# One more pair of gate tiles in the seven-product form, one third of the attention steps without a gate slice, and a new place for the copies of turned probabilities in those steps

## The reference

```
z = x @ w["w_in"]                     # 1024 x 6416
gq, gk, gv, gr, ga, sq, sk, sv, mq, gl = jnp.split(z, SPLIT_AT, axis=-1)
o_b = swa_banded(q, k, v, w["swa_sinks"])      # 8 heads of 64, own chunk and 2 before
o_c = mem_attention(mq, mem_k, mem_v)          # 4 heads of 128 into 256 memory tokens
g_a, g_b, g_c = jnp.split(jax.nn.sigmoid(gl + w["b_gate"]), 3, axis=-1)
mix = (g_a * y_a + g_b * y_b + g_c * y_c) @ w["w_o"]
x = layer_norm(ALPHA * x + mix, w["ln1_g"], w["ln1_b"])
x = layer_norm(ALPHA * x + conv_ffn(x), w["ln2_g"], w["ln2_b"])
```

## Time and profile before

| what | value |
|---|---|
| time, median of 3 runs | 1750.6 us (1750.44 to 1751.13) |
| the profiled execution's own time | 1747.55 us |
| its span | 1745.4 us |
| granted TensorE clock, mean | 0.998 |
| TensorE busy with matmuls | 1722.2 us, 99% |
| VectorE busy | 1088.5 us, 62% |
| ScalarE busy | 757.8 us, 43% |
| GpSimd busy | 219.0 us, 13% |

### The profile page before, as it was taken

One profiled execution on the slowest core, in us unless ns is written; L12 is line 12 of the kernel. 1 busy time (PEld: TensorE's weight loads), 2 busy tenths in 40 slices (PEclk: granted clock), 3 DMA queues, 4 the chain that ended last, 5 costly groups with the idle time before them and its releaser, 6 DMA issues.

```text
span 1745.4 us, 31878 instructions
## 1 busy us (share of the span) xinstructions
PE 1722.2 (99%) x12185; PEld 1667.6 (96%) x12185; DVE 1088.5 (62%) x1556; ACT 757.8 (43%) x1366; POOL 219.0 (13%) x319
## 2 busy tenths in 40 slices
PE   9999999999999999999999999999999999999997
PEld 8999999999998899899998889999999999999997
DVE  6644432666645766566664788777777777554474
ACT  6433332445434555563340255444455444433342
POOL 0000000000001200000000033333333331002011
PEclk9999999999999999999999999999999999999999
DMA  5333328422436311125463232222222213875672
GB/s 165 111 109 109 122 77 256 117 71 76 138 93 206 105 46 49 52 90 147 141 203 96 80 85 85 86 73 73 73 73 74 87 58 130 269 250 171 210 234 72
DMA packets 191505, 207.84 MB, mean 119 GB/s; under 512 B 21525, under 2 KB 152406, under 8 KB 191414
## 3 DMA queue, kind: packets, MB, share of 16 engines
q1 hardware_dynamic: 189558, 200.60, 36.9%
q0 software_dynamic: 1856, 5.99, 1.0%
HBM read 157.43 MB, written 48.53 MB: 118 GB/s over the span
## 4 chain that ended last, share of the span: by engine, by line
PE 65%; DVE 3%; issue 1%; SPq 1%; DMA 1%; ACT 1%; POOL 0%; ACTq 0%; POOLq 0%; DVEq 0%
PE banks L1681 24%; PE banks L1179 10%; PE banks L1180 10%; PE banks L1181 10%; PE banks L1638 5%; PE banks L1475 1%; PE banks L1492 1%; PE banks L1487 1%; PE banks L1455 1%; PE banks L1460 1%; DMA kpad<-gates_scratch 1%; PE banks L1649 0%; DVE wo L2809 0%; PE banks L1615 0%; SPq L797 0%
## 5 line engine op out<-in xcount | busy, mean ns | idle before, releaser
L1681 PE MATMUL banks<-x_free_r,a_hi 128*128 128x256 f32 x1232 | 226.8, 282 | 0.8 <-DVE a_lo L2919 0.5
L1179 PE MATMUL banks<-act_hi,w_hi 128*128 128x352 f32 (+1 forms) x672 | 223.7, 333 | 2.3 <-DVE w_lo L2448 1.4
L1181 PE MATMUL banks<-act_hi,w_lo 128*128 128x352 f32 (+1 forms) x672 | 218.0, 324 | 0.0
L1180 PE MATMUL banks<-act_lo,w_hi 128*128 128x352 f32 (+1 forms) x672 | 217.9, 324 | 0.0
L1681 PEld LDWEIGHTS banks<-x_free_r,a_hi 128*128 128x128 f32 x1232 | 190.1, 188 | 1.3 <-DVE x_free_r L2945 0.7
L1681 PE MATMUL banks<-xs_hi,a_hi 128*128 128x274 f32 x616 | 178.8, 290 | 1.7 <-DVE xs_lo L2945 1.1
L1681 PE MATMUL banks<-xs_lo,a_hi 128*128 128x274 f32 x616 | 178.4, 290 | 0.0
L1681 PE MATMUL banks<-xs_hi,a_lo 128*128 128x274 f32 x616 | 178.3, 289 | 0.0
L1681 PE MATMUL banks<-x_free_r,a_lo 128*128 128x256 f32 x616 | 173.4, 281 | 0.0
L1180 PE MATMUL banks<-h_lo,w_hi 128*128 128x384 f32 (+1 forms) x448 | 147.3, 329 | 0.0
L1179 PE MATMUL banks<-h_hi,w_hi 128*128 128x384 f32 (+1 forms) x448 | 146.8, 328 | 0.0
(11 more groups left out here) (355 smaller groups left out, 4324.0 us busy)
## 6 DMA issues: line engine op xcount, KB each, us to landing
w_raw<-in_w_down SPq DMA_DIRECT2D x112, 256.0 KB, 3.5
w_raw<-in_w_in SPq DMA_DIRECT2D x80, 256.0 KB, 3.9
gate_in<-gates_scratch SPq DMA_DIRECT2D x24, 529.0 KB, 3.6
h_keep<-conv SPq DMA_DIRECT2D x22, 530.0 KB, 2.7
gates_scratch<-zu SPq DMA_DIRECT2D x11, 1058.0 KB, 7.1
w_raw<-in_w_up SPq DMA_DIRECT2D x44, 256.0 KB, 3.9
x_free<-in_w_up SPq DMA_DIRECT2D x44, 256.0 KB, 3.7
h_raw<-h_keep SPq DMA_DIRECT2D x22, 384.0 KB, 5.2
```

Of the source, the lines that this page charges most:

```text
L1179: pe.matmul(out, hi, b_hi, start=start, stop=False)
L1180: pe.matmul(out, hi, b_lo, start=False, stop=False)
L1181: return pe.matmul(out, lo, b_hi, start=False, stop=stop)
L1681: last = pe.matmul(out, a[j][:, k, :], x[s][j][:, k, :], start=fresh and k == 0 and n_ == 0, stop=k == 3 and n_ == 2, skip_group_check=True)
```

## The change

Three things are changed together.

1. NZ goes from 11 to 12: gate tiles 22 and 23 are computed as a twelfth unit of the z stage. `Z_LAST` carries the parity of the last unit, and the tiles behind it use the banks of the other parity.
2. The attention stage has 18 gate slices instead of 24. Six steps, `ATT_BARE`, all with a mem unit (j % 3 = 2), have none; the slices stand in the others in order, so a tile's split comes after its third slice wherever that stands. The loops over i = 1 and 2 on the three engines are written out, since the steps differ.
3. Around a bare step k the copies of unit k's turned probabilities stand one step earlier in the programs: VectorE makes its half between the mask add and the maximum of unit k+1, ScalarE its half ahead of the exponentials of unit k+1.

```diff
-NZ = 11
+NZ = 12
+Z_LAST = (NZ - 1) % 2
-Z_GATES = (12, 14, 6, 8)
+Z_GATES = (12, 14, 6, 8, 22)
+ATT_BARE = ((0, 5), (1, 2), (1, 5), (2, 2), (2, 5), (3, 2))
+ATT_FILL = [(i, j) for i in range(5) for j in range(6) if (0, 3) <= (i, j) <= (4, 2) and (i, j) not in ATT_BARE]
...
-        z_pair(NZ - 1, 0)
+        z_pair(NZ - 2, 0)
+        z_pair(NZ - 1, Z_LAST)
...
         def gate_slice_b(i, j, beside=None):
 
-            if j % 3 == 0:
-                tile_start(i + (T_GATE_B // 2 + j // 3 - 1), 1 - j // 3)
-            proj_slice(i * 6 + (PS_GATE_B + j - 3), (PS_GATE_B + j - 3) % 2, 1 - j // 3, j % 3, beside)
+            s = att_fill(i, j)
+            if s is None:
+                return
+            f = s // 3
+            if s % 3 == 0:
+                tile_start((T_GATE_B + f) // 2, f % 2)
+            proj_slice(PS_GATE_B + s, (PS_GATE_B + s) % 2, f % 2, s % 3, beside)
...
         att_steps(0, True, False)
-        with pe.Fori(1, NT // 2 - 1) as i:
+        for i in range(1, NT // 2 - 1):
             att_steps(i, False, False)
...
                     gate_out_b(i, j)
-                probs_out(k, P)
+                if (i, j) not in ATT_BARE:
+                    probs_out(k, P)
...
                 values_out(k, j % 3, c, w)
-                if j % 3 == 2:
-                    split_hi(i + (T_GATE_B // 2 + b), 1 - b)
+                next_gate(i, j)
+                if (i, j + 1) in ATT_BARE:
+                    probs_out(k + 1, P)
...
-        def max_unit(k, swa, r, par, w, nk, band):
+        def max_unit(k, swa, r, par, w, nk, band, turned=None):
...
+                if turned is not None:
+                    probs_out(turned, P)
                 dve.wait_ge(q.masked, swa + 1)
...
-                if not (first and j < 2):
+                if not (first and j < 2) and (i, j) not in ATT_BARE:
                     probs_out(k, P)
                 n = j + 2
                 w, nk = (DEC, P + DEC) if last and n >= 6 else (P, 2 * P)
-                max_unit(k + 2, i * 4 + (n - n // 3), n % 3, n % 2, w, nk, None if last and n >= 6 else mask)
+                max_unit(k + 2, i * 4 + (n - n // 3), n % 3, n % 2, w, nk, None if last and n >= 6 else mask,
+                         k + 1 if (i, j + 1) in ATT_BARE else None)
```

More of the change, by code:

```diff
@@ L81 @@
 T_GATE_B = T_MQ + 10
-T_MERGE = T_MQ + 18
-T_WO = T_MQ + 30
-T_FFN = T_MQ + 38
+T_MERGE = T_MQ + 16
+T_WO = T_MQ + 28
+T_FFN = T_MQ + 36
 PW0, PW1, PBG, PW2, PCB, PGN, PHI = 0, NF * 2, NF * 4, NF * 4 + 24, NF * 6 + 24, NF * 8 + 24, NF * 8 + 25
@@ L475, in program @@
     BRANCHES = (2, 0, 1)
-    PS_Z, PS_G, PS_GA, PS_FILL, PS_MQ, PS_MQ_B, PS_MK, PS_MV, PS_GATE_B, PS_END = 6, 9, 11, 15, 57, 60, 63, 65, 67, 91
+    PS_Z, PS_G, PS_GA, PS_FILL, PS_MQ, PS_MQ_B, PS_MK, PS_MV, PS_GATE_B, PS_END = 6, 9, 11, 15, 57, 60, 63, 65, 67, 85
     q = Semaphores(sem)
@@ L516, in fill_slice, with att_fill @@
         return sum(FILL_SLICES[:t]) + places.index(place) if place in places else None
+    def att_fill(i, j):
+        return ATT_FILL.index((i, j)) if (i, j) in ATT_FILL else None
     def z_count(n, j):
@@ L568, in raw_count @@
         if par:
-            return 384 if isinstance(c, int) and c < 2 else c * 32 + 352
+            return 448 if isinstance(c, int) and c < 2 else c * 32 + 416
         return 32 * (W0 + 1) if isinstance(c, int) and c < 2 else c * 16 + 32 * (W0 + 1)
@@ L824, in _ @@
             mem_tile(n_)
-        last = gate_loop(T_GATE_B // 2, 16, 4, gate_st2, PS_GATE_B)
+        last = gate_loop(T_GATE_B // 2, 16, 3, gate_st2, PS_GATE_B)
         def merge_tile(turn, slot, br, mp):
@@ L851, in _ @@
         merge_tile(T_MERGE // 2, 1, BRANCHES[1], 0)
-        last(3, (0,))
+        last(2, (0,))
         sp.wait_ge(q.staged, 2 * NT + 2)
@@ L855, in _ @@
         gate_back(0)
-        last(3, (1,))
+        last(2, (1,))
         for s in range(3):
-            sp.wait_ge(gate_stored[s], 16 * (10 + NFILL))
+            sp.wait_ge(gate_stored[s], 16 * (8 + NFILL))
         for k in range(12):
@@ L1297, in _ @@
         z_pair(1, 1, 1)
-        with pe.Fori(1, NZ // 2) as i:
+        with pe.Fori(1, (NZ - 1) // 2) as i:
             z_pair(i * 2, 0)
             z_pair(i * 2 + 1, 1)
-        z_pair(NZ - 1, 0)
+        z_pair(NZ - 2, 0)
+        z_pair(NZ - 1, Z_LAST)
         tile_start(1, 0)
@@ L1306, in _ @@
         for gi in range(3):
-            proj_slice(PS_Z + gi, 3 + 4 * (gi % 2), 0, gi)
+            proj_slice(PS_Z + gi, bank_a(1 - Z_LAST, gi % 2), 0, gi)
         for s in range(2):
@@ L1917, in _ @@
         z_window(1, 1)
-        with act.Fori(1, NZ // 2) as i:
+        with act.Fori(1, (NZ - 1) // 2) as i:
             z_window(i * 2, 0)
             z_window(i * 2 + 1, 1)
+        z_window(NZ - 2, 0)
         for k in range(3):
             for s in range(2):
-                z_snap(NZ - 1, 0, s, k)
+                z_snap(NZ - 1, Z_LAST, s, k)
         split_hi(1, 0, used=(q.prod_mm[1], z_count(NZ - 1, 0)))
         for s in range(2):
-            z_snap(NZ - 1, 0, s, 3)
+            z_snap(NZ - 1, Z_LAST, s, 3)
         split_hi(1, 1, used=(q.prod_mm[1], z_count(NZ - 1, 4)))
@@ L1937, in _ @@
         for gi in range(3):
-            gate_out(PS_Z + gi, 3 + 4 * (gi % 2), gi, gate_st, 0)
+            gate_out(PS_Z + gi, bank_a(1 - Z_LAST, gi % 2), gi, gate_st, 0)
             if gi == 1:
@@ L2079, in gate_out_b, with next_gate @@
         def gate_out_b(i, j):
-            gate_out(i * 6 + (PS_GATE_B + j - 3), (PS_GATE_B + j - 3) % 2, j % 3, gate_st2, i * 2 + (1 + NFILL + j // 3))
+            s = att_fill(i, j)
+            if s is not None:
+                gate_out(PS_GATE_B + s, (PS_GATE_B + s) % 2, s % 3, gate_st2, 2 + NFILL + s // 3)
+        def next_gate(i, j):
+            s = att_fill(i, j)
+            if (i, j) == (0, 2):
+                split_hi(T_GATE_B // 2, 1)
+            elif s is not None and s % 3 == 2:
+                split_hi((T_GATE_B + s // 3 + 2) // 2, s // 3 % 2)
         def att_steps(i, first, last):
@@ L2109, in _ @@
         att_steps(0, True, False)
-        with act.Fori(1, NT // 2 - 1) as i:
+        for i in range(1, NT // 2 - 1):
             att_steps(i, False, False)
@@ L2161, in _ @@
         for gi in range(3):
-            act.wait_ge(gate_stored[gi], 16 * (10 + NFILL))
+            act.wait_ge(gate_stored[gi], 16 * (8 + NFILL))
         act.wait_ge(q.k_turned, 1)
@@ L2571, in _ @@
         z_window(1, 1)
-        with dve.Fori(1, NZ // 2) as i:
+        with dve.Fori(1, (NZ - 1) // 2) as i:
             z_window(i * 2, 0)
             z_window(i * 2 + 1, 1)
+        z_window(NZ - 2, 0)
         for k in range(3):
             for s in range(2):
-                z_combine(NZ - 1, 0, s, k)
+                z_combine(NZ - 1, Z_LAST, s, k)
             if k == 0:
@@ L2781, in att_steps @@
                     split_lo(T_GATE_B // 2, 0)
-                if j % 3 == 2:
-                    split_lo(i + (T_GATE_B // 2 + j // 3), 1 - j // 3)
+                s = att_fill(i, j)
+                if (i, j) == (0, 2):
+                    split_lo(T_GATE_B // 2, 1)
+                elif s is not None and s % 3 == 2:
+                    split_lo((T_GATE_B + s // 3 + 2) // 2, s // 3 % 2)
         def branch_lo(place):
@@ L2793, in _ @@
         att_steps(0, True, False)
-        with dve.Fori(1, NT // 2 - 1) as i:
+        for i in range(1, NT // 2 - 1):
             att_steps(i, False, False)
```

## The result

| | before | after |
|---|---|---|
| median | 1751.1 us (5 executions, 1750.4 to 1754.9) | 1777.9 us (5 executions, 1772.5 to 1779.2) |
| profiled execution: own time, span | 1747.55, 1745.4 us | 1778.02, 1775.9 us |
| mean granted clock | 0.998 | 0.992 |

The account below looks back on a forecast made before the run. TensorE, busy 99% of the span, was taken as the bound. Added z unit 20.65, removed slices -23.9 and six waits of 3.5 gave +17.8 us on 1750.6: 1768.4 us, with 1761 to 1777 for 8 in 10.

Parts of the forecast that it names:

- the likeliest case: TensorE waits 2.8 to 4.2 us at the products behind each bare step, at full clock; chance 0.68.
- The z unit: In the z stage, one more unit bound by its matmuls adds 20.65 us, its loads and store costed at nothing.
- Six slices: In the attention stage, six gate slices of 3.98 to 3.99 us removed from TensorE: -23.9 us.
- The chain of 12.99 us: Handovers up to VectorE's copy of unit k+1; TensorE arrives at 9.77 and waits 3.22 us per bare step.
- GpSimd's copies: Copies after the mem scores overlap VectorE's normalisation of k+2, lengthening each wait by 0 to 1.0 us; 0.3 taken.
- No other wait: In the attention stage, the group's other steps cost nothing; no wait worth naming at bare steps' turnings or mem products.
- The clock at 1.00: Granted clock stays 1.00 through the attention stage, so clock falls add nothing to the sum.
- falling clocks: Rival: TensorE's clock falls in the waits, 3 to 9 us for one or two, up to 30 for six; chance 0.15.
- that no wait would come: Rival: the slices were idle cover and TensorE doesn't wait behind bare steps, at none 1747.3 us; chance 0.05.
- The pure back and forth of VectorE and ScalarE: Rival: in attention only this exchange sets the pace, 19.87 us per group, 1753.3 us, up to 1762; chance 0.10.

Follow-up runs that it names:

- the kernel with both copies moved: The change, with VectorE's and ScalarE's copies of the unit behind each bare step moved ahead of the next unit's normalisation and exponentials: 1753.9 us, ratio 1.0023 to before.
- only VectorE's copy was moved: The change, with VectorE's copy of the unit behind each bare step moved up, ScalarE's left behind the next unit's exponentials: 1761.3 us, ratio 1.0063 to before.

## Why the prediction was right, and where its size was off

The direction and the mechanism were right: one wait for each of five bare steps, at the line named, on the copy named. The size was too small, 17.8 us against 26.7. The median lies 0.9 us above the range given for 8 in 10 (1761 to 1777), and 1750.6 times the ratio, 1775.5 us, lies inside it; both are above the 1764 to 1773 of the likeliest case. That the time came out so near the range was in part luck: it allowed for one or two clock falls at up to 5 us each, and there were five cheaper ones. By its own steps:

- **The z unit, +20.65.** Held, 20.64 in the stores.
- **Six slices, -23.9.** Held: a group at full clock lasts 22.31 us, as 22.86 - 3.99 + 3.5 = 22.4 said.
- **The chain of 12.99 us against TensorE's 9.77, and 3.5 us of wait.** Held. VectorE's timeline of after, through the same steps:

```profile
621.94 0.69 DVE L2780 COPY prob_T<-banks 128x512 f32<-128x512 f32 x1 [0.81 <-PE banks L1482]
622.55 1.21 DVE L2752 TENSOR_REDUCE smax<-prob 128x4 f32<-128x1024 f32 x1
...
626.26 0.16 DVE L2769 TENSOR_TENSOR sden<-ssum,sexp 128x4 f32<-128x4 f32 x1 [2.11 <-ACT sexp L2061]
...
628.98 1.22 DVE L2752 TENSOR_REDUCE smax<-prob 128x4 f32<-128x1024 f32 x1
...
632.71 0.26 DVE L2769 TENSOR_TENSOR sden<-ssum,sexp 128x4 f32<-128x4 f32 x1 [2.11 <-ACT sexp L2061]
...
633.22 1.23 DVE L2774 TENSOR_SCALAR prob<-prob,srec 128x256 f32<-128x256 f32 x4
634.37 0.68 DVE L2780 COPY prob_T<-banks 128x512 f32<-128x512 f32 x1
```

  With the end of the turning at 620.81 + 1.09 = 621.90 as 0, TensorE comes to the products at 635.14 - 3.63 - 621.90 = 9.61 (9.77 forecast) and gets them at 13.24 (12.99 + 0.3 = 13.29 forecast). Both exponential handovers, 2.11 us each, are in the chain, as was said.
- **GpSimd's copies, +0.3 with up to 1.0 as the bound.** The collision is there and cheaper. In the last group, which has none of these copies, `sden` takes 0.16 us instead of 0.26 and the normalisation 1.14 instead of 1.23, and the wait is 3.44 instead of 3.63: 0.19 us. The Trainium skill's exclusive lock ("SBUF — State Buffer", section "SBUF: two separate sides"), which the page gives for some VectorE operations only, among them those with two inputs in SBUF, would at its worst have been worth the whole 1.0. Of this the trace shows 0.19 us: GpSimd's copies run from 631.76 and last 1.76 us, as in the earlier trace rows, so over `sden` and the start of the normalisation. Whether VectorE is held there by a lock or otherwise isn't shown.
- **No other wait.** This missed a place and not a size. Behind the bare step of unit 17 ScalarE lets out `vt` and the sample keys behind exponentials that a slice used to cover; 1.45 + 2.21 us stand there, 3.66 where 3.5 was counted. Moving them ahead of the exponentials took the 2.2 away in the kernel with both copies moved. The 1.4 on `vt` stayed there.
- **The clock at 1.00.** This is the step that failed, the term of the sum that was left at nothing. The forecast gave falling clocks 0.15 as a rival, 3 to 9 us for one or two, on the ground that the waits end just as a fall would begin, 3.25 us after TensorE stops by the one event of the earlier trace rows. The last wait shows that ground to be wrong: the clock fell about 2.0 us after TensorE stopped. The falls came in four of the five waits on `prob_T` and behind the pair at the sample keys. By the stretch from the products to the next turning, held against the 5.03 of the first wait or, where the stretch is another, against the same one in the kernel with TensorE kept busy, they cost 1.46 and 1.48 (6.49 and 6.51 against 5.03), 1.49 (705.14 to 720.36 against 13.73 there), 1.65 (727.62 to 737.04 against 7.77 there) and 2.44 (761.71 - 754.24 = 7.47 against 5.03): **8.5 us**. The experiment with TensorE kept busy gives 8 (4 to 12) from times alone. So the price of one fall was overstated (5 us at most, 1.5 to 2.4 measured) and their number understated.

The two profiled spans then add up: 20.65 - 23.9 + 18.0 (waits on `prob_T`) + 3.66 (sample keys) + 8.5 (clock) + 3.7 (the scatter at the memory weights) = 30.6 us, of 1775.9 - 1745.4 = 30.5. Without the scatter it is 26.9, and the medians differ by 26.7.

The rivals: that no wait would come fell with the first row of waits. The pure back and forth of VectorE and ScalarE wasn't what this change showed. With both copies moved the kernel came near its number (19.95 us a group, 1753.9 us), but its 19.87 us is no floor: with each unit's copies placed for itself a group lasts 19.18. The third part of the change did half of what it is there for: it took away a wait of 3.9 us and left one of 3.6.

Left open: why the wait of 3.63 us at 635.14 left the clock alone and one of 3.44 didn't. The five executions of after have mean clocks of 0.993 (the one of 1772.5 us) down to 0.990 (that of 1779.2), so the number or length of falls may differ from one to the next; the rows here are of one. It is as open why one of five waits of 2.17 to 2.19 us brought a fall when only VectorE's copy was moved. The Trainium skill ("TensorE: Matmul & The Clock Gate", section "Part 1: The HAM clock gate") says that the chip watches activity in a window that runs freely and that a kernel's start doesn't reset. If that is the cause, the same gap may bring a fall or not. The rows agree so far that 3.63 us passed once without a fall (635.14) and once with one (681.33); no run here puts that rule to the test.

## What to carry to other kernels

Work that fills TensorE between the steps of a chain of handovers is cover, and what it may be exchanged for is set by that chain, measured from handover to handover; the 62% of an engine that takes part in it say nothing. When such a chain has two halves on two engines, compute both, and every small copy queued behind the same long operation: the longest hides the others until it is gone. And once a forecast contains waits of TensorE of 3.5 us, price the clock behind them as a term of the sum (it fell at five of six places here), not as the end of the range.

## What the runs showed of the hardware that was not expected

- Waits of 3.44 to 3.63 us inside otherwise dense work put TensorE to 1.2 GHz in four of five cases, and two waits of 1.45 and 2.21 us, 5.1 us apart, did once. All six waits of 3.9 us in the exchange without the moved copies did. But so did one of five waits of 2.17 to 2.19 us with VectorE's copy alone moved, where a pair like the one at the sample keys did not: the length of a wait alone doesn't tell. Waits of up to 1.2 us (both copies moved) did nothing to be seen in the attention stage.
- A fall costs 1.5 to 2.4 us: the products behind the wait at half speed (1.98 us instead of 1.09) and a part of the slice after them.
- Matmuls that nobody reads, placed in the waits, made the kernel 8 us faster than with idle waits. They are still worse than not having the waits, by 14 us (1767.7 against 1753.9).
- The wait for one transfer of weights was 0.7 to 3.5 us over the profiled executions here, and 0.9 and 2.7 us in two of the same kernel. The clock fell behind some of them (0.74 over 5 us behind 2.7, 0.76 over 7 us behind 2.9, 0.66 over 5 us behind 1.8 with both copies moved). The two spans of the unchanged kernel differ by 4.6 us.
